# A large region moved to another SBUF address, and 46 of 739 subtracts moved from VectorE to GpSimd

## What is computed

```python
mod = silu(c) @ w_ada + b_ada                       # 6 rows of 2048
h = rmsnorm(x, norm_mix) * (1 + sc_a) + sh_a
p = h @ w_in                # c_q, c_kv, k_pe, q, k, v, z, b, a, gates
y_a = attention(c_q, c_kv, k_pe) @ w_o_mla
y_b = gated_delta(silu(conv(q, k, v)), z, b, a) @ w_o_gdn
x = x + gt_a * ((g_a * y_a + g_b * y_b) @ w_o)
h = rmsnorm(x, norm_ffn) * (1 + sc_f) + sh_f
gate, up = split(h @ w_gate_up)                     # 5632 each
x = rmsnorm(x + gt_f * ((silu(gate) * up) @ w_down), final_norm)
u, v, gate = split(rmsnorm(x, a_norm) @ a_w_in_2)   # 4096 each
y = gelu(u) * (w_s (per group) @ rmsnorm(gelu(v)) + b_s)
out = rmsnorm(x + (y * silu(gate)) @ a_w_out_2, final_norm_2)
```

## Time and profile before

| | |
|---|---|
| median of 3 runs | 2233.59 us (2232.49 to 2233.64) |
| the profiled execution, its own time | 2233.74 us |
| its span | 2232.1 us |
| PE busy | 2189.5 us, 98% |
| PE weight loads | 1830.0 us, 82% |
| DVE busy | 1504.2 us, 67% |
| ACT busy | 1007.6 us, 45% |
| POOL busy | 24.2 us, 1% |
| read from memory | 503 MB, 226 GB/s over the span |

### The profile page before, as it was taken

How to read it: one execution, slowest core, us unless ns; L and a number is a source line. 1 busy time by engine, 2 the same in 40 slices (tenths; PEclk the granted TensorE clock), 3 DMA queues, 4 the chain that set the end, 5 groups by cost and what they waited for, 6 DMA issues and landing times.

```text
span 2232.1 us, 27221 instructions
## 1 busy us (share of the span) xinstructions
PE 2189.5 (98%) x10552; PEld 1830.0 (82%) x10552; DVE 1504.2 (67%) x1891; ACT 1007.6 (45%) x1284; POOL 24.2 (1%) x26
## 2 busy tenths in 40 slices
PE   6899999999999999999999999999999999999998
PEld 5788988888888888888888888878888888888887
DVE  8989698988788677755455555576556655655556
ACT  5356445434444644443444334464444444444444
POOL 0001000000000000000000000000000000000000
PEclk9999999999999999999999999999999999999999
DMA  9975577877998678865666566665666666566663
GB/s 404 419 269 157 181 232 252 292 256 238 335 346 291 218 266 292 295 218 183 196 190 188 182 196 189 187 205 182 191 196 188 189 193 195 184 190 192 193 189 129
DMA packets 241552, 507.08 MB, mean 227 GB/s; under 512 B 19304, under 2 KB 34960, under 8 KB 235920
## 3 DMA queue, kind: packets, MB, share of 16 engines
q1 hardware_dynamic: 241424, 505.35, 69.1%
HBM read 503.16 MB, written 2.12 MB: 226 GB/s over the span
## 4 chain that ended last, share of the span: by engine, by line
PE 84%; DVE 8%; DMA 3%; issue 2%; ACT 2%; POOL 0%; DVEq 0%; SPq 0%; ACTq 0%; POOLq 0%
PE bank L1240 26%; PE bank L1242 26%; PE bank L1241 26%; DVE WL L2064 3%; PE bank L1172 2%; PE bank L1431 1%; DVE RAW L2051 1%; PE bank L1247 1%; PE bank L1248 1%; PE bank L1249 1%; DVE A L2241 1%; DMA RAW<-in_w_cd_dram 1%; DMA RAW<-in_w_ada_dram 1%; DMA A<-in_w_cq_dram 1%; DMA RAW<-in_w_cq_dram 1%
## 5 line engine op out<-in xcount | busy, mean ns | idle before, releaser
L2064 DVE TENSOR_TENSOR WL<-RAW,WH 128x1024 fp32r<-128x1024 f32 x706 | 860.4, 1223 | 585.4 <-ACT WH L1514 574.3
L1514 ACT CAST WH<-RAW 128x1024 fp32r<-128x1024 f32 x706 | 741.6, 1054 | 850.2 <-PE bank L1242 721.8
L1240 PE MATMUL bank<-WH,HTh 128*128 128x512 f32 x1922 | 757.7, 394 | 0.9 <-DVE WL L2064 0.9
L1242 PE MATMUL bank<-WH,HTl 128*128 128x512 f32 x1922 | 749.3, 390 | 0.0
L1241 PE MATMUL bank<-WL,HTh 128*128 128x512 f32 x1922 | 747.8, 389 | 0.0
L1242 PEld LDWEIGHTS bank<-WH,HTl 128*128 128x128 f32 x1922 | 360.7, 188 | 76.7
L1240 PEld LDWEIGHTS bank<-WH,HTh 128*128 128x128 f32 x1922 | 361.0, 188 | 75.6 <-DVE WL L2064 2.2
L1241 PEld LDWEIGHTS bank<-WL,HTh 128*128 128x128 f32 x1922 | 361.1, 188 | 72.7
L1240 PE MATMUL bank<-WH,R2h 128*128 128x512 f32 x408 | 160.6, 394 | 0.7 <-DVE WL L2064 0.6
L1242 PE MATMUL bank<-WH,R2l 128*128 128x512 f32 x408 | 159.1, 390 | 0.0
L1241 PE MATMUL bank<-WL,R2h 128*128 128x512 f32 x408 | 158.8, 389 | 0.0
(11 more groups left out here) (301 smaller groups left out, 1824.1 us busy)
## 6 DMA issues: line engine op xcount, KB each, us to landing
RAW<-in_a_w_in_dram SPq DMA_DIRECT2D x192, 512.0 KB, 3.8
RAW<-in_w_gate_up_dram SPq DMA_DIRECT2D x176, 512.0 KB, 4.5
RAW<-in_w_ada_dram SPq DMA_DIRECT2D x128, 512.0 KB, 5.6
RAW<-in_w_in_dram SPq DMA_DIRECT2D x112, 512.0 KB, 5.1
RAW<-in_w_down_dram SPq DMA_DIRECT2D x88, 512.0 KB, 4.3
RAW<-in_a_w_out_dram SPq DMA_DIRECT2D x64, 512.0 KB, 3.8
A<-in_w_ada_dram SPq DMA_DIRECT2D x17, 1024.0 KB, 14.0
RAW<-in_w_o_dram SPq DMA_DIRECT2D x32, 512.0 KB, 6.1
```

The lines of the kernel that those rows point to most:

```text
L1240: e.matmul(o, ah[:, s], hi[:, k, :], start=first, stop=False)
L1242: i = e.matmul(o, al[:, s], hi[:, k, :], start=False, stop=last)
L1514: e.copy(hi, rv).then_inc(S["hi"], 1)
L2064: e.tensor_tensor(lo, rv, hi.bitcast(F32), ALU.subtract).then_inc(S["lo"], 1)
```

## The change

Two things. First, `Layout` places A and ROPE right behind RAW, and CST, MOD, CB and ST behind them: A moves down by 16800 bytes, the four small tensors up by 103680. All tensors over A move with it. Second, the subtract of some halves is done by POOL: for the jobs conv, z, ga, gb, wo and gate the third and seventh of eight halves, for om and og the third of four, but not for conv 0 and gate 1 to 10 (conv 1 has two halves only). These are 46 of 739. They have a semaphore of their own, `lo_pool`, and PE and the raw slot's next transfer wait for whichever engine did the half.

```diff
@@ Layout.__init__
         self.RAW = self.place("RAW", NR * 1024)
+        self.abase = self.at
+        self.A = self.place("A", 100 * KB)
+        self.ROPE = self.place("ROPE", 320)
         self.CST = self.place("CST", C_END)
         self.MOD = self.place("MOD", 96)
         self.CB = self.place("CB", 2048)
...
-        self.abase = self.at
-        self.A = self.place("A", 100 * KB)
-        self.ROPE = self.place("ROPE", 320)
@@ tables
+POOL_LOWS = {n: (2, 6) for n in ("conv", "z", "ga", "gb", "wo", "gate")} | {n: (2,) for n in ("om", "og")}
+DVE_LOWS = [("conv", 0)] + [("gate", c) for c in range(1, 11)]
@@ Schedule.front_split
         self.halves.append((j, t0, nkt, i, c0, width))
+        by = "lo_pool" if (t0 // j.step) in POOL_LOWS.get(j.name, ()) and (j.name, j.c) not in DVE_LOWS else "lo"
+        self.lows[by] = self.lows.get(by, 0) + 1
+        self.low_of.append((by, self.lows[by]))
...
-        self.marks[("raw_free", self.raw_slot(i))] = (("lo", hid + 1),)
+        self.marks[("raw_free", self.raw_slot(i))] = (self.low_of[hid],)
@@ pe_program
-            W.wait_ge("lo", hid + 1)
+            W.wait_ge(*sch.low_of[hid])
@@ dve_program
-        elif kind == "split":
+        elif kind == "split" and sch.low_of[args[0]][0] == "lo":
@@ pool_program
+        if kind == "split" and sch.low_of[args[0]][0] == "lo_pool":
+            hid, = args
+            j, _, nk, i, c0, width = sch.halves[hid]
+            rv = L.raw(sch.raw_slot(i), nk, width)[:, :, c0:c0 + j.n]
+            hi, lo = L.halves(sch.place[hid], nk, j.n)
+            W.wait_ge(f"raw{sch.raw_slot(i) % NR1}", sch.raw_value[i])
+            W.wait_ge("half", sch.after[hid])
+            if sch.place[hid] >= NHL and j.x != "ht":
+                W.wait_ge(*extra_free(sch, sch.place[hid]))
+            W.wait_ge("hi", hid + 1)
+            e.tensor_tensor(lo, rv, hi.bitcast(F32), ALU.subtract).then_inc(S["lo_pool"], 1)
```

More of the change, by code:

```diff
@@ L355, in __init__ @@
         self.marks = {}
+        self.lows, self.low_of = {}, []
         self.build()
@@ L2656, in pool_program @@
         kind, args = step[0], step[1:]
-        if kind == "x_rs":
+        if kind == "split" and sch.low_of[args[0]][0] == "lo_pool":
[9 more added lines that the diff above has]
+            e.tensor_tensor(lo, rv, hi.bitcast(F32), ALU.subtract).then_inc(S["lo_pool"], 1)
+        elif kind == "x_rs":
             power(L.rs1, L.rs1, 2, args[0])
```

## The result

The changed kernel takes 2245.05 us (median of 4 runs, 2243.09 to 2248.18) against 2233.15 us (4 runs, 2232.49 to 2233.64) of the kernel before: a ratio of 1.0055 [1.004, 1.007], 11.9 us slower. I had forecast 2224.1 us, and the range ended at 2239. The profiled execution shown here is the slowest of the four, 2248.18 us, with a span of 2246.6.

What follows compares the result with a forecast made beforehand. The prediction took the rate at which PE takes matmuls from its queue as the bound. The move of A (-8.5) and DVE's relief (-1.0) gave -9.5 us, from 2233.59 to 2224.1 us, range 2220 to 2239.

Steps and rivals of the forecast that it cites:

- The move of A: Matmuls reading A, mostly down, drop from 233.3 to 226.7 ns once A starts on the 128-byte grid: -8.5 us.
- Rival (a): A's height in memory, not its offset, slows matmuls; aTh stays at 233 ns: 2234 us; 0.28 shared with a cancelled gain.
- The POOL subtract: Each of the 46 moved subtracts takes 2.4 us on POOL, between 1.22 and 2.8, against 1.22 on DVE.
- Its cover: Time between a half's cast and PE taking it hides POOL's later end; tightest room 2.9 and 2.5 us; costed at 0.
- my own sign: PE waiting for POOL anywhere would mean that the cover was too small.
- The gain: DVE rid of 46 subtracts, thirteen between 280 and 448 us, so PE waits less for its queue: 1.0 us.
- My ceiling: At most the 3.5 us that PE waits for DVE between 280 and 450 us can be gained by relieving DVE.
- rival (b): POOL and DVE block each other on memory reads: 8 us reach PE; 2232 with offset gain, 2242 without (slower outcomes 0.17).
- the likeliest case: Offset reading holds with little harm by POOL: 2220 to 2229 us, likeliest 2224; chance 0.55.
- its signature: Some DVE subtracts at 2 to 4 us, with PE waits for WL over 3.5 us between 280 and 450 us.
- The condition: Blocking decides as soon as DVE loses more than 1.22 us per POOL subtract.
- the slower case: Blocking without the offset gain, or a POOL subtract much longer than 2.8 us: around 2242 us; chance 0.17.

Runs made afterwards that it cites:

- A high on the grid: The kernel before with 96 unused bytes ahead of A, so A stays high but starts on a multiple of 128 bytes: 2225.54 us.
- the early 26: The changed kernel with only the 26 subtracts of conv, om, ga, z and gate on GpSimd, the others back on DVE: 2241.7 us.
- the kernel whose GpSimd only writes: The changed kernel, but in the 46 places GpSimd fills WL with zeros twice instead of subtracting and reads nothing: 2217.09 us.

## Why the prediction was wrong

**The move of A** was right in mechanism and size. Forecast -8.5, measured -8.1 (A alone), with 249 matmuls in 56 us as named, and 226.7 ns for those that read WHx. Rival (a), height, is refuted by A high on the grid.

**The POOL subtract** was right: 2.4 us taken, median 2.40. Its cover was "Costed at 0", and is right to within 0.7 us, what PE waits for POOL. (By my own sign any such wait means that it was too small; the kernel with the early 26 alone has 2.1 us.)

**"The gain: ... I take 1.0"** is wrong in size. Where GpSimd locks nothing, the relief gives 7.6 us. My ceiling was the 3.5 us of waits that name DVE. But the windows in the earlier trace rows had 1.80 + 0.92 + 1.74 = 4.5 us of idle PE, and from 160 to 785 us there are 7.1 in all, 2.0 of them between 160 and 224, outside the stretches I read. A ceiling has to come from the idle time, and the waits tell only part of its cause.

**The step that failed is rival (b)'s price**, and with it the likeliest case. The mechanism stood there, with half of its signature: DVE subtracts of 2 to 4 us came (one takes 3.41). The other half, PE waits for WL of over 3.5 us between 280 and 450 us, did not: there DVE ends 1.2 us of them, 1.6 in the kernel without a subtract on GpSimd. The long waits are for other results of DVE, up to 4.0 us. The condition, that DVE loses more than 1.22 us per POOL subtract, came true barely: 1.29.

I priced it as a queue: 13 x 1.2 = 15.6 us of more work for DVE against 13.9 us of its idle time, half of it to PE, 8 us, in 280 to 448 us alone. The runs show 20.3 us net, and against the kernel whose GpSimd only writes 28. Four things differ.

- The queue sum itself gives nothing. A subtract costs DVE 1.29 us and relieves it of 1.07, 0.2 us more and not 1.2, and DVE is busy 144.6 us of these 168 in the changed kernel against 153.2 without a subtract on GpSimd (a part of the work slips behind the stretch). By its load DVE didn't become the bound.
- DVE's idle time covers nothing: in the changed kernel DVE idles 9.0 and 13.5 us in the first two of these windows, while PE waits for it. A hold falls on one operation, and when PE has nothing queued but what needs that one, it stands still (L2211 at 300.46 us: 2.43 us, then 4.0 us of wait, where the same wait is 1.2 without).
- The stretch was too short: in the changed kernel the second of the moved subtracts, from 156.30 to 158.69 us, already holds a 32-column product of DVE (L1966) for 2.40 us, and by 174 us PE, level with the kernel before until 164, is some 2 us behind it.
- PE's clock fell, which no term had: 6.5 us.

With 8 replaced by 20, (b) beside the offset gain gives 2244 to 2245 instead of 2232. The 2242 named for the slower case needed (a) to be true; that it lies near 2245 is luck.

I also gave (b) too little chance. The Trainium skill (SBUF — State Buffer, Who interferes with whom) says that a DVE instruction with two SBUF inputs and a GpSimd instruction that reads SBUF exclude each other, that the later one fully blocks, and that one which only writes does not contend with it. The trace agrees in each point: 3.41 us against 1.22, and 1279 ns beside fills. The page also says that tensor_scalar can take a mode that contends; L2211 with one tensor operand, 2.43 us for two against 0.58, agrees, and so do its 0.80 us beside a fill.

## What to carry to other kernels

Before moving work to an idle GpSimd, look at what DVE does meanwhile, and not at how long GpSimd takes: if GpSimd reads SBUF, each of its operations can hold up one DVE operation for nearly its whole length (2.2 of 2.4 us here), and the price is set by who waits for that one. The same subtract cost 0.65 us in the part with attention and the cells and 0.05 us or nothing later on, so DVE's busy share or total idle time gives no price. Relief of a loaded engine can come from the order of the work: ten products later in the program gave 4.8 us, where the subtracts on GpSimd cost 20.3.

## What the runs showed of the hardware

- 128x512 matmuls of which one operand starts 32 or 64 bytes off a multiple of 128 in SBUF follow each other 6.6 ns further apart: 242 or 243 in 56 us where there are 249, and 7.3 to 8.9 us of this kernel. It doesn't depend on how high the operand lies.
- GpSimd subtracts 128x1024 fp32 in 2.40 us and copies it in 1.21 (medians; the shortest copy 1.04), and fills it in 0.955. The two that read stretch to as much as 3.45 and 2.14 us when DVE is at work as they start (3.45 at 236.30 us, with a modulation product of DVE from 236.25); either engine can be the one that waits.
- A GpSimd that only writes, 88 us in all, leaves DVE's operations with two operands in SBUF at their times (1279 ns against 1278). A tensor_scalar pair was held by a fill twice, by 0.25 us.
